# Position table of the first mixer: stored 128 times and read with a pitch one element shorter, in place of a product that turns the partitions over

## The reference

```python
rel_own = qpos[:, None] - (n_past * MOBA_BLOCK + offs)[None, :]
logit_own = (jnp.einsum('bhqd,bhkd->bhqk', qc, k_own) * scale
             + bias_h[:, t5_bucket(rel_own)])
logit_own = jnp.where(rel_own >= 0, logit_own, NEG_INF)
```

## Time and profile before

| | us |
|---|---|
| median of 3 runs | 1020.79 (1020.69 to 1020.94) |
| the profiled execution, its whole time | 1020.92 |
| the profiled execution, first to last instruction (span) | 1019.1 |
| PE busy | 1001.6 |
| DVE busy | 683.8 |
| ACT busy | 503.0 |

### The profile page before, as it was taken

One profiled execution on the slowest core, in us unless ns is written; L12 is line 12 of the kernel. 1 busy time (PEld: TensorE's weight loads), 2 busy tenths in 40 slices (PEclk: granted clock), 3 DMA queues, 4 the chain that ended last, 5 costly groups with the idle time before them and its releaser, 6 DMA issues.

```text
span 1019.1 us, 20189 instructions
## 1 busy us (share of the span) xinstructions
PE 1001.6 (98%) x8766; PEld 950.1 (93%) x8766; DVE 683.8 (67%) x1089; ACT 503.0 (49%) x663; POOL 3.0 (0%) x8
## 2 busy tenths in 40 slices
PE   9999999999999999999999999999999999999997
PEld 8898989999999888879999999999887899999997
DVE  6868576776555887865665555588967576555555
ACT  6476664344444653554644343465536364444433
POOL 0000000000000000000000000000000000000000
PEclk9999999999999999999999999999999999999999
DMA  9435435454544232222555454543221254554531
GB/s 331 177 116 196 142 133 198 169 206 167 194 179 155 89 114 105 85 77 106 183 193 204 166 203 170 186 159 107 92 95 74 78 208 170 175 197 168 204 125 42
DMA packets 24024, 156.41 MB, mean 153 GB/s; under 512 B 2608, under 2 KB 3936, under 8 KB 6400
## 3 DMA queue, kind: packets, MB, share of 16 engines
q1 hardware_dynamic: 21888, 151.70, 40.9%
q10 hardware_dynamic: 1840, 2.50, 0.7%
q0 software_dynamic: 208, 0.92, 0.3%
HBM read 154.05 MB, written 1.06 MB: 152 GB/s over the span
## 4 chain that ended last, share of the span: by engine, by line
PE 86%; DVE 7%; ACT 4%; issue 2%; DMA 1%; SPq 0%; ACTq 0%; DVEq 0%
PE bank L464 72%; DVE w_lo L1639 2%; ACT w_hi L1185 2%; DVE arena L1621 1%; PE bank L899 1%; DVE x L1621 1%; PE bank L904 1%; PE bank L915 1%; DMA x<-in_x 1%; ACT h_hi L1218 1%; PE bank L1123 1%; DVE h_lo L1694 1%; PE bank L1153 1%; DVE arena L2100 1%; DVE h_lo L1646 0%
## 5 line engine op out<-in xcount | busy, mean ns | idle before, releaser
L464 PE MATMUL bank<-h_hi,w_hi 128*128 128x256 f32 x1480 | 425.6, 288 | 6.0 <-DVE w_lo L1639 3.1
L1639 DVE TENSOR_TENSOR w_lo<-raw,w_hi 128x2048 fp32r<-128x2048 f32 (+3 forms) x144 | 323.1, 2250 | 156.1 <-ACT w_hi L1185 155.4
L464 PE MATMUL bank<-h_lo,w_hi 128*128 128x256 f32 x1480 | 418.6, 283 | 0.0
L464 PE MATMUL bank<-h_hi,w_lo 128*128 128x256 f32 x1480 | 418.5, 283 | 0.0
L1185 ACT ACTIVATE w_hi<-raw 128x2048 fp32r<-128x2048 f32 (+1 forms) x145 | 270.0, 1867 | 78.7 <-PE bank L464 77.1
L464 PEld LDWEIGHTS bank<-h_hi,w_hi 128*128 128x128 f32 x1480 | 283.4, 192 | 16.8 <-DVE h_lo L1694 4.6
L464 PEld LDWEIGHTS bank<-h_lo,w_hi 128*128 128x128 f32 x1480 | 283.6, 192 | 0.9 <-issue 0.7
L464 PEld LDWEIGHTS bank<-h_hi,w_lo 128*128 128x128 f32 x1480 | 283.6, 192 | 0.0
L464 PE MATMUL bank<-mix_hi,w_hi 128*128 128x256 f32 x720 | 207.0, 288 | 2.2 <-DVE mix_lo L1621 1.4
L464 PE MATMUL bank<-mix_lo,w_hi 128*128 128x256 f32 x720 | 203.7, 283 | 0.0
L464 PE MATMUL bank<-mix_hi,w_lo 128*128 128x256 f32 x720 | 203.7, 283 | 0.0
(11 more groups left out here) (305 smaller groups left out, 844.0 us busy)
## 6 DMA issues: line engine op xcount, KB each, us to landing
raw<-in_w SPq DMA_DIRECT2D x136, 1024.0 KB, 4.8
raw<-in_w SPq DMA_DIRECT2D x5, 512.0 KB, 3.7
raw<-in_w SPq DMA_DIRECT2D x2, 896.0 KB, 4.5
raw<-in_w SPq DMA_DIRECT2D x2, 768.0 KB, 4.1
cst<-in_consts SPq DMA_DIRECT2D x1, 1184.0 KB, 10.4
arena<-bias_rows ACTq DMA_DIRECT2D x1, 1024.0 KB, 7.6
out<-arena ACTq DMA_DIRECT2D x4, 256.0 KB, 2.1
mat<-in_mat POOLq DMA_DIRECT2D x2, 384.0 KB, 3.4
```

The lines of the kernel that those rows point to most:

```text
L464: last = pe.matmul(dst, w[a](k), act[b](k), start=start and i == 0 and j == 0, stop=stop and i == n - 1 and j == 2, skip_group_check=loose)
L1639: dve.tensor_tensor(w_lo[:, s, 0:n], raw[:, s, 0:n], w_hi[:, s, 0:n].bitcast(F32), ALU.subtract)\
```

## The change

The scratch tensor gets 128 copies of each of the 8 rows, one after the other: 8 x 128 x 384 numbers instead of 8 x 384. One DMA stores them, whose source names each of the 8 rows 128 times (a step of 0 in the middle dimension). The load then reads with a pitch of 383 from partition to partition. Partition p so takes copy p from element 127-p on, and the table lands in `bias` in the right order. The four products with `flip` go away, as do the four copies on ACT, the tile `hankel` and the constant `flip` (128 columns of the constants).

The waits move too. PE no longer waits for `rel_in`. It waits for `rel_out` (the store) ahead of `gla_scores`, since the arena under `relrow` is written again from there on. ACT waits for `rel_out` after it has copied chunk 6, in the place where it copied the bias, and issues the load there. DVE waits for `rel_in` ahead of the first logits.

```diff
--- before.py
+++ after.py
@@ -144,7 +144,6 @@
     out = {"ident": np.eye(P), "ones": np.ones((P, P)), "freq": freq}
     out["bones"] = block_ones(64)
     out["gla_mask"] = block_ones(64) * (i[:, None] <= i[None, :])
-    out["flip"] = np.eye(P)[::-1]
 
     out["before"] = np.stack([i[:, None] < i[None, :], i[:, None] <= i[None, :]], 1).reshape(P, 2 * P)
 
@@ -299,7 +298,7 @@
         B1 |= area(at_products, dict(att=(TT, 512), st=(3, T), go=(2, T), gt=(2, T), att_l=(4, 384),
                                      att_p=(2, 384)))[0]
 
-        REL, _ = area(at_products, dict(onehot=(384,), relrow=(384,), relneg=(384,), hankel=(8, T)))
+        REL, _ = area(at_products, dict(onehot=(384,), relrow=(384,), relneg=(384,)))
 
         B2, at2 = area(0, dict(
             pm=(9, T), a=(2, T), kkn=(2, T), gate=(2, T), kp=(2, T), kr=(2, 2, 2, P), bh=(2, T), kh=(2, T),
@@ -340,7 +339,7 @@
         positions = sem("positions_loaded")
         mats, first_mats = sem("mixer_matrices_loaded"), sem("first_mixer_matrices_loaded")
         bias_tables = sem("bias_tables_loaded")
-        rel_out, rel_in = sem("bias_row_stored"), sem("bias_hankel_loaded")
+        rel_out, rel_in = sem("bias_row_stored"), sem("bias_loaded")
         stored = sem("output_stored")
         V = Steps(sem("vector_step"), plan.get("V"))
         A = Steps(sem("scalar_step"), plan.get("A"))
@@ -687,18 +686,11 @@
                                          B1["lru"][:, 0, t * T:(t + 1) * T], start=True, stop=True)
                 last.then_inc(M.sem, M.mark("lru_gates"))
                 project(l, 4)
-                pe.wait_ge(rel_in, 16)
+                project(l, 5)
+
                 pe.wait_ge(late_tables, 16)
-                for i in range(4):
-                    if i >= 2:
-                        pe.wait_ge(A.sem, A.at("bias", i - 2))
-                    pe.matmul(bank[2 + i % 2][:, :], C("flip"),
-                              REL["hankel"][:, 2 * i:2 * i + 2, :].rearrange("p a b -> p (a b)"),
-                              start=True, stop=True).then_inc(M.sem, M.mark("bias", i))
-                project(l, 5)
-
+                pe.wait_ge(rel_out, 16)
                 pe.wait_ge(V.sem, V.at("gla_ke"))
-                pe.wait_ge(A.sem, A.at("bias", 3))
                 for t in range(TT):
                     last = pe.matmul(bank[2 + t][:, :].rearrange("p (h t) -> p h t", h=4), B1["kd"][:, t * P:(t + 1) * P],
                                      B1["qm"][:, :, t * P:(t + 1) * P], start=True, stop=True)
@@ -1323,9 +1315,8 @@
                     last = act.activation(B1["ke"][:, s], B1["g2"][:, s], ACT.Exp, scale=-1 / 16, bias=small[:, n:n + 1])
                 last.then_inc(A.sem, A.mark("gla_ee"))
                 hi_of(CHUNK[l, "in", 6])
-                for i in range(4):
-                    act.wait_ge(M.sem, M.at("bias", i))
-                    copy(B1["bias"][:, 2 * i:2 * i + 2, :], pairs(2 + i % 2)).then_inc(A.sem, A.mark("bias", i))
+                act.wait_ge(rel_out, 16)
+                act.dma_start(B1["bias"], ins["bias"]).then_inc(rel_in, 16)
                 hi_of(CHUNK[l, "in", 7])
                 act.wait_ge(M.sem, M.at("gla_turn"))
                 copy(flat(B1["keT"]), bank[6][:, 0:T]).then_inc(A.sem, A.mark("gla_turned"))
@@ -1558,10 +1549,11 @@
 
                     hi_of(CHUNK[0, "in", 3])
                     act.wait_ge(V.sem, V.at("rel_row"))
-                    act.dma_start(rel_scratch, REL["relrow"][0:8, :]).then_inc(rel_out, 16)
+
+
+                    act.dma_start(rel_scratch, REL["relrow"][0:8, :].unsqueeze(1).broadcast_to([8, P, 384]))\
+                        .then_inc(rel_out, 16)
                     hi_of(CHUNK[0, "in", 4])
-                    act.wait_ge(rel_out, 16)
-                    act.dma_start(REL["hankel"], ins["hankel"]).then_inc(rel_in, 16)
                 block1() if l == 0 else rwkv(l)
 
                 gain, c0 = "pre_ffn" if l == 0 else f"ffn{l}", CHUNK[l, "gu", 0]
@@ -1901,6 +1893,7 @@
                     for j in heads:
                         probabilities(l, j)
 
+                dve.wait_ge(rel_in, 16)
                 logits_of(0, 1)
                 lo_of(CHUNK[l, "out", 0])
                 probs_of(0, 1)
@@ -2424,9 +2417,9 @@
         ins = {name[3:]: nc.dram_tensor(name, a.shape, mybir.dt.from_np(a.dtype), kind="ExternalInput").ap()
                for name, a in arrays.items()}
         ins["pos"] = ins["pos"].broadcast_to([P, T])
-        scratch = nc.dram_tensor("bias_rows", [8, 384], F32, kind="Internal")
+        scratch = nc.dram_tensor("bias_rows", [8, P, 384], F32, kind="Internal")
         ins["scratch"] = scratch.ap()
-        ins["hankel"] = bass.AP(scratch, 0, [[1, P], [384, 8], [1, T]])
+        ins["bias"] = bass.AP(scratch, P - 1, [[383, P], [P * 384, 8], [1, T]])
         out = nc.dram_tensor("out", [P, KT * T], F32, kind="ExternalOutput").ap()
         return nc, program(nc, ins, out, plan)
```

## The result

The changed kernel takes 1031.08 us (median of 4 runs, 1030.68 to 1032.65) against 1020.87 for the kernel before in runs on the same chip: a ratio of 1.0102, 95% interval 1.0089 to 1.0114. It is 10.2 us slower. 1027.6 was forecast, with a range of 1017.0 to 1031.5. The profiled executions took 1030.68 and 1020.92 us, with spans of 1028.9 and 1019.1: 9.8 us between them.

What follows compares the result with a forecast made beforehand. PE was taken as the bound, busy 1001.6 of 1019.1 us. The store lands at 23.53 + 4.0 + 29.6 + 1.8 = 58.9, holding `gla_scores` by 6.8 us: 1020.79 + 6.8 = 1027.6, range 1017.0 to 1031.5.

Steps and rivals of the forecast that it cites:

- What is removed: Products with `flip` on PE between steps 4 and 5: 3.53 us off the chain; the ACT copies worth nothing by themselves.
- Two shares: Store transfer from 8 partitions: two sixteenths of 426 GB/s, 53 GB/s, so 29.6 us; this forecast got 55%.
- the extreme: Rival for the store: all rows share one sixteenth, 26.6 GB/s, 59 us of transfer; kernel time 1055; chance 4%.
- two kinds of limit: What sets the store's rate: SBUF's side, held likelier, or the engines' own rate (eight engines, 213 GB/s, 7.4 us).
- the picture of turns: Store beside weight loads: queues alternate on an engine, a store row every 366 ns instead of 231; 3.6 us lost.
- the 1.8 of the sum: Store slowed beside the weights: half of the 3.6 us loss, taken between turns and no loss.
- The cover of the weights: Chunk 6 under the store: landed at 31.8, taken by ACT at 37.72, so 5.9 us of cover.
- The rival with the blocked weights: Store blocks weights on its engines, chunk 6 lands about 59, step 6 at 63.3: +9.0 us, 1029.8; chance 8%.
- a transfer of 26 us: Upper end of the in-between store case, transfers of 21 to 26 us: 1017.5 to 1022.8 us; chance 6%.
- 0.27 and half of 0.06: Chance of faster by over 0.2%: fast store (27%) and half of the in-between cases (6%), given as 0.29.
- the price of the hold: PE at `gla_scores`: waits for the store's landing at 58.9 where it started at 52.15, +6.8 us.
- Who else stands behind the waits: After the landing: ACT's sigmoid has 2 us of cover, chunk 7 and the table load are hidden; nothing on top.

Runs made afterwards that it cites:

- Four other placements: Changed kernel with rows stored from every fourth partition, partitions 0 to 15, every second, every eighth: 1017.81, 1017.84, 1017.95 and 1018.13 us.
- the two fillers: Changed kernel with 29 or 24 products of no use on PE ahead of the wait for the store: 1030.21 and 1028.80 us.

## Why the prediction was right, and where it was off

The direction and the mechanism held: the store is the price, it lands long after PE could go on, and PE stands at `gla_scores`.

- **What is removed.** PE came to the end of step 5 at 48.84 (48.6 forecast). Where nobody is held the kernel gains 2.8 to 3.2 us (3.2 to 3.3 forecast). The wait of 0.2 us at step 6 was foreseen; that step 6 takes 6.02 in place of 5.75 us behind a wait was not.
- **The store's rate.** Two shares was a choice that no row supported, a softening of the extreme by a factor of two. Of the two kinds of limit it named the right one; that the factor was right too is luck as far as the rows go. Four other placements now bear it out. The size of the share was off: 48 GB/s for both in the place of 53, so 32.5 us of transfer in the place of 29.6.
- **The store beside the weights.** Here the picture of turns failed. In 28 to 42 us the store goes on at nearly its full rate, and it is the weights that wait. The views don't part the engines, but half of the chunk on the free half of the engines fits the numbers. In 28 to 32 us SP's queue moves only half of chunk 6, and that chunk, issued at 27.0, lands after 19.3 us (4.7 before):

```profile
q10 hardware_dynamic: 127, 0.20, 43.4%
q1 hardware_dynamic: 72, 0.52, 38.6%
```

```profile
raw<-in_w SPq DMA_DIRECT2D x1, 1024.0 KB, 19.3
```

Where weights do get through the store slows, to 181 rows in 8 us instead of 252 at the steady rate (42 to 50 us):

```profile
q1 hardware_dynamic: 253, 1.88, 59.1%
q10 hardware_dynamic: 181, 0.28, 10.2%
```

That is some 2 us lost, but 26 to 28 us (95 packets) and 50 to 54 us (153 packets, 126 at the steady rate) gave about as much back, so that it resembles the 1.8 of the sum only by chance. The first row moved at 26.2, 2.6 us after the issue, and the landing came 33.5 us later. The sum had at most 4.0 us for start and landing and 31.4 for the rest. So its total of 35.4 us is near the 36.2 measured because the 4.0 was too much where the transfer was too little.

- **The cover of the weights.** 5.9 us were forecast for chunk 6, with a landing at 31.8. It landed at 46.3, and it cost nothing only because DVE's split of it comes after the small work of softplus anyway, at 48.59 before and 48.64 now. The copy ended at 48.26, so 0.4 us were left. The rival with the blocked weights was half right: they were held, but came free before the store ended. Two slips of the prediction that change nothing: by its own rule a transfer of 26 us gives 1022.2, not 1022.8, and 0.27 and half of 0.06 make 0.30, not 0.29.
- **The step that failed: the price of the hold.** The sum priced it as its length alone, 6.8 us. The chain shows 7.51 for the hold (the landing came 0.9 us later than the 58.9 forecast), and 2.03 + 0.21 = 2.24 us on top in `gla_scores` and `gla_turn`. Of these 1.97 are the lower clock and 0.27 the start after a wait, as the two fillers show. 7.51 + 2.24 = 9.75 of the 9.8 us between the profiled executions. The other 0.4 us of the medians lie in how the runs of the changed kernel scatter, which is only argued.
- **Who else stands behind the waits.** No one: step 6 was followed by its next product without a wait, and the load, 7.0 us, was there long before the logits at 95.29.

## What to carry to other kernels

A store that repeated a few rows was here as fast as the paths behind the partitions that held them, not as its bytes: count the groups of four partitions (with those 32 apart as one), before the engines. Making the rows on spread partitions cost nothing here, as the product that made them had the columns to spare. And price a hold of TensorE by its length plus what runs at the lower clock behind it, and add the 0.27 us that a start after a wait took here at the full clock; a wait placed where nobody stands behind it made even the slow store free.

## What the runs showed that I had not expected

Weights queued beside a slow store can stand still for 10 us and more: chunk 6 was issued at 27.0, SP's queue had moved half of it by 32, and it landed at 46.3. The engines count as busy meanwhile, though they move little: in 32 to 34 us the store's 48 GB/s are 43% of the 16 engines' time. A high DMA share at few GB/s was here the sign of a starved path. With 16 partitions on 16 engines (86.3% at 97 GB/s) no weights moved at all in 28 to 38 us, and ACT could take chunk 6 only at 45.7 us, after the store had landed at 43.1, and the kernel still took 1017.84. Why weights pass at 42 us and not at 30 no run tells.
